# Reloading the token rows in eight pieces, moving a weight split and a mask pattern ahead, and 64-row skip products

## What is computed

```python
def reference(...):                       # the names of the second block end in _2
    h = concat([meta_tokens, x])          # 16 + 512 rows
    # first block
    mix = merged(conv branch, stick-breaking attention, gates) @ w_out
    h = h + rms_norm(mix, g_post_mix)     # h is the block's own input
    h = h + rms_norm(conv_gated_mlp(rms_norm(h, g_pre_ffn)), g_post_ffn)
    # second block
    u, z_s, q_lat, kv_lat, k_rope, z_m, gl_s, gl_m = split(norm(x) @ w_in)
    # S5 state-space branch, 64 groups of 16 channels, 64 states each:
    # s_t = A s_(t-1) + B u_t ;  y_t = Re(C s_t) + D * u_t
    y_s = ((glu_a * sigmoid(glu_b)) * silu(z_s)) @ w_br_ssm
    # latent attention, 16 heads, rotary keys, block-causal in chunks of 64
    q  = rms_norm(q_lat) @ w_q_up ;  kv = rms_norm(kv_lat) @ w_kv_up
    y_m = (attend(q, kv, k_rope) * silu(z_m)) @ w_br_mla
    x = x + gate * rms_norm((sigmoid(gl_s) * y_s + sigmoid(gl_m) * y_m) @ w_out)
```

## Time and profile before

| | |
|---|---|
| median of three runs | 2083.61 us (2078.96 to 2084.55) |
| the profiled execution | 2086.71 us |
| its span (first to last instruction) | 2085.0 us |
| mean granted TensorE clock | 0.937 of full speed |
| weight transfers | 271 of 512 KB, 3.5 us from issue to landing (median) |
| the load of H | 2112 KB, 8.2 us |
| one transfer for the mask's positions | 256 KB, 3.8 us |

### The profile page before, as it was taken

How to read it: one execution, slowest core, us unless ns; L and a number is a source line. 1 busy time by engine, 2 the same in 40 slices (tenths; PEclk the granted TensorE clock), 3 DMA queues, 4 the chain that set the end, 5 groups by cost and what they waited for, 6 DMA issues and landing times. The chain is left out here.

```text
span 2085.0 us, 31580 instructions
## 1 busy us (share of the span) xinstructions
PE 1934.9 (93%) x12232; PEld 1686.0 (81%) x12232; DVE 1078.7 (52%) x1500; ACT 854.9 (41%) x1135; POOL 199.7 (10%) x329
## 2 busy tenths in 40 slices
PE   5999999999899988899999979699979999999996
PEld 5999999999899977799998857476757777778884
DVE  4434444433333324655542247999666776754543
ACT  4645555554422223333332224133346556543331
POOL 0100001000000000000000004777200000000000
PEclk8899999999899989999999989678889999999998
DMA  3121222122222233132233226311211212133331
GB/s 116 61 61 61 72 69 72 56 64 70 61 91 91 91 124 110 58 94 91 91 94 98 91 72 160 59 36 33 58 47 50 81 56 80 55 96 108 120 109 78
DMA packets 64501, 165.93 MB, mean 80 GB/s; under 512 B 21808, under 2 KB 21936, under 8 KB 64304
## 3 DMA queue, kind: packets, MB, share of 16 engines
q1 hardware_dynamic: 64432, 164.98, 25.9%
HBM read 154.20 MB, written 8.39 MB: 78 GB/s over the span
## 5 line engine op out<-in xcount | busy, mean ns | idle before, releaser
L1597 DVE TENSOR_TENSOR WL<-WR,WH 128x1024 fp32r<-128x1024 f32 x271 | 335.7, 1240 | 303.4 <-ACT WH L1169 294.2
L1169 ACT ACTIVATE WH<-WR 128x1024 fp32r<-128x1024 f32 x271 | 284.3, 1053 | 216.0 <-PE J L894 78.9
L702 PE MATMUL J<-XH,WH 128*128 128x264 f32 (+1 forms) x1376 | 295.0, 297 | 18.2 <-DVE XL L1601 18.0
L702 PE MATMUL J<-XL,WH 128*128 128x264 f32 (+1 forms) x1376 | 289.2, 293 | 0.0
L702 PE MATMUL J<-XH,WL 128*128 128x264 f32 (+1 forms) x1376 | 288.6, 292 | 0.0
L702 PEld LDWEIGHTS J<-XH,WH 128*128 128x128 f32 x1376 | 225.8, 199 | 23.6 <-issue 17.1
L702 PEld LDWEIGHTS J<-XL,WH 128*128 128x128 f32 x1376 | 224.3, 198 | 0.0
L702 PEld LDWEIGHTS J<-XH,WL 128*128 128x128 f32 x1376 | 223.4, 198 | 0.0
L2220 POOL TENSOR_SCALAR_AFFINE_SELECT E<-E 128x128 f32<-128x128 f32 (+1 forms) x160 | 45.0, 319 | 502.6 <-DVE E L1648 344.5
L923 PE MATMUL J<-X2H,WH 128*128 128x512 f32 x168 | 69.8, 416 | 8.8 <-DVE X2L L1878 8.8
L2242 POOL TENSOR_TENSOR SM<-SM 128x32 f32<-128x32 f32 x15 | 4.6, 309 | 728.3 <-DVEq L1912 727.2
(11 more groups left out here) (417 smaller groups left out, 4472.3 us busy)
## 6 DMA issues: line engine op xcount, KB each, us to landing
WR<-weights SPq DMA_DIRECT2D x271, 512.0 KB, 3.5
X<-tokens SPq DMA_DIRECT2D x4, 528.0 KB, 5.3
H<-tokens SPq DMA_DIRECT2D x1, 2112.0 KB, 8.2
res_dram<-H SPq DMA_DIRECT2D x1, 2048.0 KB, 8.1
u_dram<-UT SPq DMA_DIRECT2D x8, 256.0 KB, 2.2
US<-u_dram SPq DMA_DIRECT2D x16, 128.0 KB, 6.0
gate_dram<-GST SPq DMA_DIRECT2D x8, 256.0 KB, 2.2
GSB<-gate_dram SPq DMA_DIRECT2D x8, 256.0 KB, 3.6
```

Source lines behind the costliest of these rows:

```text
L702: mm = pe.matmul(o[:, 512 * h:512 * h + half], ws[:, s, w], xs[:, a:a + half], start=(k == 0 and i == 0), stop=(k == 7 and i == 2))
L1169: act.activation(WH[:, n % SPLIT, :], WR[:, n % RAW, :], ACT.Copy).then_inc(w_hi, 1)
L1597: dve.tensor_tensor(WL[:, n % SPLIT, :], WR[:, n % RAW, :], WH[:, n % SPLIT, :].bitcast(F32), ALU.subtract).then_inc(w_lo, 1)
```

## The change

Three edits. (1) SP loads H in eight pieces of 264 KB, one tile each. Two weight jobs are issued ahead of each piece, beginning with `N_OUT+2` and `N_OUT+3`, which now stand ahead of the wait for the gates' jobs. DVE waits for all eight pieces where it waited for one. (2) The mask pattern gets a tile of its own, `PAT`, and POOL writes it as soon as the last turned output of the state-space branch is made. ACT makes its eight copies ahead of the latent norms. The split of job `N_LAT+7` moves ahead of the second latent norm on ACT and on DVE. (3) `DD` has 128 partitions and is filled in two halves by two DVE operations. The skip product takes 64 partitions, those of its group, where it took 16; the identity's columns for that half select the 16 rows that count.

```diff
@@ -294,6 +294,7 @@
         M2H, M2L = tile2("M2H", 2), tile2("M2L", 5)
         F3 = tile2("F3", 0, F32)
         RES = tile2("RES", 6, F32)
+        PAT = sb("PAT", [P, 2, S2], V[7])
 
 
         def places(start, end):
@@ -336,7 +337,7 @@
         place, at7 = places(after_setup, M2)
         YT = place("YT", [P, SUB, PT_, GP])
         TK = [tk0, sb("TK1", [P, GT, P], V[5])]
-        DD = place("DD", [GP, GROUPS, GP])
+        DD = place("DD", [P, GROUPS, GP])
         CPR = [place("CPR0", [P, PT_, SUB + 1, GP]), sb("CPR1", [P, PT_, SUB + 1, GP], V[6])]
         CPI = [place("CPI0", [P, PT_, SUB + 1, GP]), sb("CPI1", [P, PT_, SUB + 1, GP], c1_at)]
         K1 = place("K1", [P, PT_, SUB + 1, GP])
@@ -559,14 +560,18 @@
 
             stream(0, N_OUT + 2)
 
-            sp.wait_ge(job_done, N_OUT)
-            sp.dma_start(H[:].rearrange("p (m t) -> p m t", m=DT), x_view).then_inc(h_landed, 16)
             def load_one(n):
                 s = n % RAW
                 sp.wait_ge(w_lo, val(n - RAW + 1))
                 sp.dma_start(WR[:, s, :], weights[n]).then_inc(w_landed[s], 16)
 
-            stream(N_OUT + 2, N_U)
+            for m in range(DT):
+                load_one(N_OUT + 2 + 2 * m)
+                load_one(N_OUT + 3 + 2 * m)
+                if m == 0:
+                    sp.wait_ge(job_done, N_OUT)
+                sp.dma_start(H[:, m * L1:(m + 1) * L1], x_view[:, m]).then_inc(h_landed, 16)
+            stream(N_UP + 2, N_U)
             for m in range(3):
                 load_one(N_U + m)
 
@@ -948,7 +953,7 @@
                 pe.wait_ge(read_out[slot(t + 1)], nth(t + 1))
                 pe.wait_ge(cp_ready, val(m + 1))
                 if m == 0:
-                    pe.wait_ge(dd_ready, 1)
+                    pe.wait_ge(dd_ready, 2)
                 for g in range(GT):
                     pr, r = g // 2, half_rows(g % 2)
                     for x, (bb, cp) in enumerate(((BBR, CPR[m % 2]), (BBI, CPI[m % 2]))):
@@ -957,7 +962,7 @@
                         mm = pe.matmul(J[(t + 1) % 2][0:GP, at:at + P], bb[r, PT_ * m + pr],
                                        cp[r, pr, 0:SUB].rearrange("p i q -> p (i q)"),
                                        start=x == 0, stop=False, skip_group_check=True)
-                    mm = pe.matmul(J[(t + 1) % 2][0:GP, at:at + GP], IDENT[0:GP, 0:GP], DD[:, GT * m + g],
+                    mm = pe.matmul(J[(t + 1) % 2][0:GP, at:at + GP], IDENT[r, r.start:r.start + GP], DD[r, GT * m + g],
                                    start=False, stop=True, skip_group_check=True)
                 mm.then_inc(g_done, 1)
 
@@ -1452,7 +1457,15 @@
 
                     act.wait_ge(trig_in, 4)
                     act.activation(TAB[:], TAB[:], ACT.Sin, scale=PRM[:, a_sgn:a_sgn + 1]).then_inc(trig_out, 1)
+            act.wait_ge(pattern, 6)
+            for x in range(2):
+                act.activation(Q2H[x][96:P], PAT[96:P, 0], ACT.Copy)
+                act.activation(Q2L[x][96:P], PAT[96:P, 0], ACT.Copy, scale=0.0)
+                act.activation(K2H[x][96:P], PAT[96:P, 1], ACT.Copy, scale=MASKED)
+                act.activation(K2L[x][96:P], PAT[96:P, 0], ACT.Copy, scale=0.0).then_inc(kr_hi, 1)
             for k in range(4):
+                if k == LATT:
+                    split_hi(N_LAT + 7)
                 if k % LATT == 0:
                     root(5 + k // LATT, S2)
                 act.wait_ge(xf_ready, val(3 * DT + k + 1))
@@ -1460,16 +1473,9 @@
                 act.activation(dst[:, k % LATT * S2:(k % LATT + 1) * S2], [CT, VT][k % 2][:, 0:S2], ACT.Copy)\
                    .then_inc(xh_ready, 1)
 
-            split_hi(N_LAT + 7)
             act.wait_ge(rope_ready, 1)
             for x in range(2):
                 act.activation(K2H[x][64:96], RO[0:32], ACT.Copy).then_inc(rope_hi, 1)
-            act.wait_ge(pattern, 6)
-            for x in range(2):
-                act.activation(Q2H[x][96:P], PB[96:P, 0], ACT.Copy)
-                act.activation(Q2L[x][96:P], PB[96:P, 0], ACT.Copy, scale=0.0)
-                act.activation(K2H[x][96:P], PB[96:P, 1], ACT.Copy, scale=MASKED)
-                act.activation(K2L[x][96:P], PB[96:P, 0], ACT.Copy, scale=0.0).then_inc(kr_hi, 1)
 
             def attend(m):
                 n, t, h = N_ATT + 4 * m, T_ATT + 8 * m, 2 * m
@@ -1787,7 +1793,7 @@
                     dve.tensor_tensor(H[:, s], H[:, s], tmp, ALU.add).then_inc(h_ready, 1)
 
             r = root(1, Q_MIX + DT, HALFK)
-            dve.wait_ge(h_landed, 16)
+            dve.wait_ge(h_landed, 16 * DT)
             add_normed(F, L1, g_mix, r, 0, LIVE)
             r = root(2, Q_PREF + DT, HALFK)
             dve.wait_ge(h_ready, DT)
@@ -1955,9 +1961,11 @@
             for k in range(2):
                 link(dve.memset(SR[k][:, :, 0:1], 0.0))
                 link(dve.memset(SI[k][:, :, 0:1], 0.0))
-            dve.tensor_tensor(DD[:], IDENT[0:GP, 0:GP].unsqueeze(1).to_broadcast([GP, GROUPS, GP]),
-                              PRM[0:GP, a_d:a_d + GROUPS].unsqueeze(2).to_broadcast([GP, GROUPS, GP]),
-                              ALU.mult).then_inc(dd_ready, 1)
+            for x in range(2):
+                r, w = slice(64 * x, 64 * x + 64), [64, GROUPS, GP]
+                dve.tensor_tensor(DD[r], IDENT[r, 64 * x:64 * x + GP].unsqueeze(1).to_broadcast(w),
+                                  PRM[r, a_d:a_d + GROUPS].unsqueeze(2).to_broadcast(w),
+                                  ALU.mult).then_inc(dd_ready, 1)
             dve.memset(TK[0][:], 0.0).then_inc(tk_zeroed, 1)
             for k in range(2):
                 dve.wait_ge(u_stored[k], 16 * DT // 2)
@@ -2057,8 +2065,8 @@
             link(rope(J[(T_LAT + 4) % 2][:, 0:S2]))
             dve.nop().then_inc(read_out[(T_LAT + 4) % 2], 1)
             dve.tensor_tensor(RO[0:64], RO[0:64], R2[0:64], ALU.add).then_inc(rope_ready, 1)
+            split_lo(N_LAT + 7)
             latent(LATT, root2(6, Q_KV + LATT, 256))
-            split_lo(N_LAT + 7)
             dve.wait_ge(rope_hi, 2)
             for x in range(2):
                 ins = low(K2L[x][64:96], RO[0:32], K2H[x][64:96])
@@ -2311,11 +2319,11 @@
                 pool.wait_ge(cp_ready, m + 1)
 
 
-            pool.wait_ge(xl_ready, 3 * DT + 2 * LATT)
-            pool.memset(PB[:], 0.0).then_inc(pattern, 1)
+            pool.wait_ge(yt_turned, DT)
+            pool.memset(PAT[:], 0.0).then_inc(pattern, 1)
             pool.wait_ge(pattern, 1)
             for x in range(2):
-                v = PB[:, x].rearrange("p (i h t) -> p i h t", i=4, h=2)[:, :, x]
+                v = PAT[:, x].rearrange("p (i h t) -> p i h t", i=4, h=2)[:, :, x]
                 pool.memset(v, 1.0).then_inc(pattern, 1)
                 pool.wait_ge(pattern, 2 + 2 * x)
                 pool.affine_select(out=v, in_=v, compare_op=ALU.is_equal, fill=0.0, base=96,
```

## The result

The changed kernel takes 2060.47 us (median of 4 runs, 2055.38 to 2062.88), beside 2084.08 (2078.96 to 2087.38) for the kernel before on the same chip: ratio 0.9882, 95% interval 0.9855 to 0.9910. Timed again on another occasion it took 2058.54 against 2087.20, ratio 0.9859 (0.9843 to 0.9875). So 24 to 29 us are gained where 21.2 were forecast. The profiled execution has a span of 2061.2 us (before 2085.0).

A forecast was written before the change was run, and what follows sets the result against it. PE, busy 93% of the span, was taken as the bound, so only its time or waits count. Parts 1, 3 and 2 gave 12.8 + 6.4 + 2 = 21.2 us; 2083.6 - 21.2 = 2062.4, range 2055.5 to 2070.5 (8 in 10).

The forecast's parts named there:

- the stall: Output projection: PE idles 9.86 us before its eighth block because H's load holds back a weight, its split and the tile.
- the ring: State-space loop: PE's output products, POOL's six C operations, kernel G, next output products; G lies on it whole.
- Rivals 2 and 3: 2: H's pieces delay weights, 7 us lost, 2069.4, chance 0.05; 3: eighth block waits for something else, 2078.6, chance 0.05.
- The stall changed its name: Before attention: PE's 8.06 us wait for the gate's split nearly goes, but some 9.6 us idle stay before the key product.
- The pause: Kernel G: PE's pause before each skip product, with the weight load idle too; removing it gains 0.13 to 0.17 us a group.
- rival 1: Kernel G: the pause before the skip product stays, part 3 gives 0, time 2068.8; chance 0.17.
- groups of 0.55 and 0.95 us: Kernel G: a group's time in the new form at full and half clock, from 0.68 and 1.12.
- PE's waits for CPI unchanged: State-space loop, ahead of G: PE's waits for POOL's CPI stay near 1 us.
- My bound of 0.24: Kernel G: most a group could gain, 0.68 - 0.44 us with only wide products left, 11.5 us in all.
- The cap of 9 us: State-space loop: upper bound of part 3; beyond about 9 us PE would wait for DVE instead.
- rival 4: State-space loop, wait before line 1006: DVE becomes the bound, PE falls to half clock every m, 34 us, time 2096; chance 0.03.
- The lead of 10.7 us: State-space loop: DVE's seventh state is done at 1477.60, its reader starts at 1488.32; would shrink to near 3 us.

The follow-up runs named there:

- order_even_odd: Against the changed kernel: kernel G's groups ordered 0, 2, 4, 6, 1, 3, 5, 7, so neighbours share a half of the partitions; loop 181.6 us, changed kernel 181.5.
- padded_groups: Against the changed kernel: G's groups ordered 0, 2, 4, 6, 1, 3, 5, 7 and each group's CPR product issued twice; loop 184.4 us.
- pool_light: Against the changed kernel: POOL's six B and six C operations left out for m = 2 to 7, so old tables are used; loop 146.2 us.

## Why the prediction was right, and where it was not

**What bounds the kernel.** Right for the stall (the transfer, the split, the tile) and for the ring: DVE's states lay 6.9 to 11.7 us ahead of their readers in six of the eight m.

**Part 1, forecast 12.8 us, measured 11 to 13.** Each step came as told: the split of N_OUT+2 ends 3.4 us ahead of SP's issue (forecast 744.45 less 741, 3.5), the tile 3.2 us behind it (3.1), no idle time in PE, no fall of the clock, and the further pieces held nothing up (68.5 us in every kernel that has them). Rivals 2 and 3 are out.

**Part 2, forecast 2 us, measured 1 to 2.** The stall changed its name, as told: 9.25 us ahead of the key product (forecast 9.6). The later up-projection runs at full clock where it ran at half, as told: it takes 1.36 us from its first start to the first score, 2.72 before.

**Part 3, forecast 6.4 us, measured 13 to 16.** This is the term that was mis-sized. The pause was seen rightly, and rival 1, that it stays, is out. Three steps failed, and three signs that the prediction named with them: groups of 0.55 and 0.95 us, PE's waits for CPI unchanged, and a lead of near 3 us left to DVE.

1. The group. I took 0.55 and 0.95 us, from 0.68 and 1.12. Without two groups at once it takes 0.48 (order_even_odd), so the pause was worth 0.20 rather than 0.13. My bound of 0.24 gained, "only wide products left", assumed besides that products of two groups never overlap; they do, and a group takes 0.28.
2. The clock, the larger one. I counted G's groups at the two clocks as they stood, and never asked whether the clock comes down inside G. It does, in every one of the six later calls: rows of the kernel before show full clock at G's start and half at its end. Six calls took 42.8 us where 48 groups of 0.68 would take 33. 51.0 us of the loop at half clock begin in G before, none in the changed kernel, 10.2 in padded_groups. padded_groups, with groups of 0.70 us, gained 12.5 us, where its calls of G are only 7.0 us shorter. That this is the clock's doing is read from these rows; no run changes the clock alone. The granted clock from the first SI to the last YT was 0.81 before, 0.94 in padded_groups and 0.93 in the changed kernel.
3. The cap of 9 us. It rested on "DVE can't come earlier". From the first SI to the last, DVE was busy for 129.50 us before and for 122.80 after, with nearly the same operations (160 and 161): they met POOL's at other times. The stage's 15.4 us add up at DVE: the last YT follows the last SI by 2.8 us where it was 7.6 (4.8); DVE's wait for Z of m = 7 is gone (4.8); its operations are 6.7 shorter; the second diagonal costs 0.9 (forecast 0.8). 4.8 + 4.8 + 6.7 - 0.9 = 15.4. The 6.7 is made up of more and less: of the 98 operations on 128x256 with both inputs in SBUF 55 took longer than 0.42 us before and 43 after (together 90.2 and 77.9 us), while the scans took 4.1 us more, the copies of MT 3.2 more and the weight splits 1.8 less. What shifted these meetings with POOL wasn't worked out.

That DVE becomes the bound in every m is the place that rival 4 named, and it came true: eight waits, 30.2 us. Its price did not: from m = 1 on the clock fell in only two of the seven waits, those of 6.04 us, while the others (three of 0.9, then 2.8 and 1.3 us) left it at full. The wait of 11.5 us stands before the first output products, where PE had waited 4.4 us before; G of m = 0 and 1, which stand ahead of it, got 9.7 us shorter. The lead of 10.7 us was used up whole, where the prediction's last part left near 3.

**The sum.** 12.8 + 2 + 6.4 = 21.2 was forecast. The profiled pair shows 12.8 + 2.2 + 15.4 = 30.4 in the three stages, of the 30.9 from H's issue on; the medians show 23.6 and 28.7, with an untouched first stretch that varies by more than any single term. The forecast of 2062.4 lay 1.9 us from the median of the first comparison and 3.9 from that of the second; that it came so near, with a term 9 us too small, is in part the luck of that stretch. It was 7.1 us longer in the profiled pair and, going by the medians, took back about as much of the gain there.

## What to carry to other kernels

A small product of another tile shape inside a chain of larger ones is dear: look in the trace for idle weight loads ahead of it, and for a clock that is full at the block's start and half at its end, for then what follows the block pays too. Keep one tile shape through a block, or gather the odd ones at its end. And before you cap a gain by another engine's lead, ask what sets that engine's own pace: here DVE's operations got shorter in sum because they met POOL's at other times. Compare stages between common events, not totals, where untouched work varies by nearly as much as the gain (18 us here).

## What the runs showed of the hardware

- Matmuls of 64 rows in the lower and upper half of the partitions run at the same time when they alternate in the program: eight groups in 2.26 us, against 3.72 with the same products ordered by half.
- A 16-row product between 64-row ones costs about 0.20 us per group of three, at full clock (0.68 against 0.48 in order_even_odd). Eight of them together behind the 64-row ones make a call only 0.1 us longer than eight 64-row ones in their places (2.35 against 2.26).
- PE counts as busy for the whole of a G call before (7.30 of 7.30 us) at a granted clock of 0.66; with the pauses filled it is 5.50 of 5.50 at 1.00 in five of six calls. A busy share of 100% didn't keep the clock up: it fell inside all 30 of G's later calls with the old skip product, in five profiles.
- DVE's fp32 operation on 128x256 takes 0.42 us with an input in PSUM whatever POOL does. With two inputs in SBUF it takes 0.42 beside an idle POOL (all 98 in pool_light); with POOL busy for some two thirds of the time, 55 of 98 took longer in the kernel before, 1.3 us in the mean.
